# Moving the split tokens of a two-layer decoder trunk to multiples of 2048 bytes in SBUF

## The reference

```
for i in range(DEPTH):                       # DEPTH = 2
    y = swa_sink_attention(x, ...) if i % 2 == 0 else forgetting_attention(x, ...)
    x = layer_norm(ALPHA * x + y, ln_g[i, 0], ln_b[i, 0])
    h = causal_conv3(x @ w_up[i]) + conv_b[i]          # 2048 -> 2 * 5632 columns
    y = (silu(h[:, :5632]) * h[:, 5632:]) @ w_down[i]  # 5632 -> 2048 columns
    x = layer_norm(ALPHA * x + y, ln_g[i, 1], ln_b[i, 1])
```

## Time and profile before

| | |
|---|---|
| median of 3 runs | 2227.64 us (2227.63 to 2227.85) |
| profiled execution, its own time | 2227.25 us |
| its span, first to last instruction | 2225.4 us |
| TensorE busy | 2194.1 us (99%) |
| VectorE, ScalarE, GpSimd busy | 1336.2, 1039.6, 219.6 us |
| mean granted clock of TensorE | 0.996 |
| DMA queue of the weights | 385.92 MB, 56.5% of 16 engines |

### The profile page before, as it was taken

The page is one execution under the profiler, slowest core; times in us unless marked ns, Lnnn a source line. Parts: engine busy times, 40 slices in busy tenths (PEclk is TensorE's granted clock), DMA queues, the critical chain, the costliest instruction groups (busy, mean ns, idle before and its releaser), DMA issues.

```text
span 2225.4 us, 40894 instructions
## 1 busy us (share of the span) xinstructions
PE 2194.1 (99%) x15265; PEld 2027.2 (91%) x15265; DVE 1336.2 (60%) x1805; ACT 1039.6 (47%) x1380; POOL 219.6 (10%) x206
## 2 busy tenths in 40 slices
PE   8999999999999999999999999999999999999996
PEld 7998899999999988888899998899999999988885
DVE  5566576666666554446665665576666566654445
ACT  4554365454545443335444444364545454543332
POOL 2000002310000000000240330001230000000001
PEclk9999999999999999999999999999999999999998
DMA  8444556666666655555655654656666666665553
GB/s 262 152 149 157 180 163 206 199 198 188 187 186 187 187 188 188 189 186 158 189 183 163 203 172 140 196 160 196 201 203 187 188 188 188 186 225 187 187 188 104
DMA packets 206952, 408.71 MB, mean 184 GB/s; under 512 B 12652, under 2 KB 13756, under 8 KB 206620
## 3 DMA queue, kind: packets, MB, share of 16 engines
q1 hardware_dynamic: 200192, 385.92, 56.5%
q0 software_dynamic: 5776, 21.34, 3.1%
q10 hardware_dynamic: 908, 0.43, 0.1%
HBM read 405.46 MB, written 2.18 MB: 183 GB/s over the span
## 4 chain that ended last, share of the span: by engine, by line
PE 94%; DVE 3%; DMA 1%; ACT 1%; issue 0%; SPq 0%; ACTq 0%; DVEq 0%
PE ps L1176 19%; PE ps L1179 18%; PE ps L1178 18%; PE ps L1162 11%; PE ps L1164 11%; PE ps L1163 11%; PE ps L1304 1%; PE ps L1311 1%; DVE w_lo L749 1%; PE ps L1322 1%; PE ps L1323 1%; PE ps L1303 1%; PE ps L1321 0%; DMA raw<-in_a_w_qkv_dram 0%; DMA raw<-in_b_w_qkvf_dram 0%
## 5 line engine op out<-in xcount | busy, mean ns | idle before, releaser
L749 DVE TENSOR_TENSOR w_lo<-raw,w_hi 128x1024 fp32r<-128x1024 f32 x728 | 924.4, 1276 | 662.5 <-ACT w_hi L471 662.0
L471 ACT ACTIVATE w_hi<-raw 128x1024 fp32r<-128x1024 f32 x728 | 771.6, 1060 | 989.0 <-PE ps L1179 550.5
L1176 PE MATMUL ps<-xh,w_lo 128*128 128x256 f32 x3572 | 1006.3, 282 | 2.4 <-DVE xl L790 1.7
L1179 PE MATMUL ps<-xh,w_hi 128*128 128x256 f32 x3572 | 996.2, 279 | 0.0
L1178 PE MATMUL ps<-xl,w_hi 128*128 128x256 f32 x3572 | 996.2, 279 | 0.0
L1176 PEld LDWEIGHTS ps<-xh,w_lo 128*128 128x128 f32 x3572 | 671.7, 188 | 5.4 <-DVE xl L790 3.1
L1178 PEld LDWEIGHTS ps<-xl,w_hi 128*128 128x128 f32 x3572 | 671.9, 188 | 0.4
L1179 PEld LDWEIGHTS ps<-xh,w_hi 128*128 128x128 f32 x3572 | 671.4, 188 | 0.0
L1164 PE MATMUL ps<-w_hi,hid_h 128*128 128x512 f32 x704 | 278.4, 396 | 0.0
L1162 PE MATMUL ps<-w_lo,hid_h 128*128 128x512 f32 x704 | 278.4, 396 | 0.0
L1163 PE MATMUL ps<-w_hi,hid_l 128*128 128x512 f32 x704 | 278.4, 396 | 0.0
(11 more groups left out here) (164 smaller groups left out, 1501.1 us busy)
## 6 DMA issues: line engine op xcount, KB each, us to landing
raw<-in_ffn_w_up_dram SPq DMA_DIRECT2D x352, 512.0 KB, 3.6
raw<-in_ffn_w_down_dram SPq DMA_DIRECT2D x176, 512.0 KB, 4.4
raw<-in_b_w_qkvf_dram SPq DMA_DIRECT2D x96, 512.0 KB, 4.2
raw<-in_a_w_qkv_dram SPq DMA_DIRECT2D x40, 512.0 KB, 4.3
raw<-in_a_w_o_dram SPq DMA_DIRECT2D x32, 512.0 KB, 4.5
raw<-in_b_w_o_dram SPq DMA_DIRECT2D x32, 512.0 KB, 4.6
bias<-rel_by_distance POOLq DMA_DIRECT2D x4, 1024.0 KB, 6.6
bias<-minus_cumulated_decay POOLq DMA_DIRECT2D x4, 1024.0 KB, 6.8
```

The costliest lines, as they stand in the source:

```text
L471: act.activation(w_hi[:, loc % RING], raw[:, loc % RING], ACT.Copy).then_inc(high_ready, 1)
L749: dve.tensor_tensor(w_lo[:, s], raw[:, s], w_hi[:, s].bitcast(FP32), ALU.subtract).then_inc(low_ready, 1)
L1176: pe.matmul(o, w_lo[:, slot, k % 2, cols], xh[:, k, :], start=(k == 0 and j % 2 == 0), stop=False, skip_group_check=True)
L1179: last = pe.matmul(o, w_hi[:, slot, k % 2, cols], xh[:, k, :], start=False, stop=(k == KT - 1), skip_group_check=True)
```

## The change

One tile of 408 float32 per partition (1632 bytes) is declared behind `warm` and ahead of `xh`. Nothing reads or writes it.

More of the change, by code:

```diff
@@ L154, in trunk @@
         warm = sb("warm", [P, 1])
+        sb("fill", [P, 408])
         with ExitStack() as first:
```

## The result

| | before | after |
|---|---|---|
| median of the runs | 2227.70 us | 2245.49 us (2245.38 to 2245.62) |
| ratio, 95% interval | | 1.008 [1.0064, 1.0096] |
| span of the profiled execution | 2225.4 us | 2243.8 us |
| TensorE busy | 2194.1 us | 2213.0 us |
| VectorE, ScalarE busy | 1336.2, 1039.6 us | 1336.9, 1039.1 us |

The forecast was 2227.6 us with a range of 2168 to 2232. The first answer of the profile after is its busy times, which answer to the earlier trace rows.

What follows compares the result with a forecast made beforehand. The prediction took TensorE to bound the kernel, busy 2194.1 of 2225.4 us. All terms were 0: 2227.25 us of the profiled execution + 0, with the runs' median 0.4 us above, gave 2227.6 us, range 2168 to 2232.

Steps and rivals of the forecast that it cites:

- the small matmuls: Attention and transposes, an estimated 1000 matmuls: aligned or not they take the same, 0 us, bounds +-3 us.
- the step of 3.33 ns between neighbouring paces: Turned matmuls (256 moving columns): one cycle more per 32 columns, 36 for 35; used for the upper bound, +58.2 us.
- Reads of the big matmuls: Operand reads of 10752 turned (256 moving columns) and 3360 512-column matmuls: start addresses cost nothing, 0 us.
- rival 3: 14112 big matmuls: with both operands at 0 modulo 128, weight load strikes the moving read's memory; +58.2 us, 2285.8; chance 0.14.
- Rival 1: Big matmuls: reads clash less when starts differ by a multiple of 64, 34 cycles not 35; gain 58.2 us, 2169.4; chance 0.14.
- Rival 2: Big matmuls: the offset of 32 makes float32r slower than its columns; gain 130 us, 2098 us; chance 0.05.

Runs made afterwards that it cites:

- the bench: Runs of matmuls alone on idle memory, no layers computed, in stretches differing in operand starts, columns, types or leading matmuls; 256 moving columns at distance 0 took 120.0 ns.
- m1: Float32r matmuls alone on idle memory instead of the layers, 70 stretches of 48 with varied operand starts and columns; 256 moving columns took 120.0 ns at distance 0.
- e5: Against the kernel before: unused tiles of 160 bytes ahead of `xh` and 64 bytes ahead of `oh`; 2176.35 us, ratio 0.977.
- e2: Unused tile ahead of `xh` of 1760 bytes instead of the changed kernel's 1632 (distance 0 in both kinds); 2240.47 us, ratio 1.0055 to the kernel before.

## Why the prediction was wrong

**What held.** TensorE sets the time, no instruction changed, and VectorE, ScalarE and the small matmuls don't mind the addresses. After the change VectorE's and ScalarE's busy times are within 0.7 us of before, and the spacings of the small matmuls add up to the same within 0.1 us. The count of the big matmuls and their pace of before were right, and the step of 3.33 ns between neighbouring paces is a real one.

**The step that failed: "Reads of the big matmuls", taken as 0.** It measured +18.3 us (19.0 through the means): 20.8 lost on the turned matmuls, 2.5 gained on the others. The 0 rested on two readings of rows.

The first was that the extra cycles grow with the moving columns (24 for 256, 48 for 512), so that they are a share and not a price of a start. The two numbers are right, but the proportion was chance: the kernel had distance 32 with 256 columns and 224 with 512, which happen to give 24 and 48. In the bench the proportion holds at distance 32 by itself, and not at others: distance 224 has 28 and 48, distance 0 has 32 for both lengths (120.0 and 226.7 ns) and distance 192 has 16 and 48. Two points at two different distances were read as one law.

The second was the gate's products: the first eight at the pace of the turned matmuls, then 113 ns. I took the change of pace under equal addresses for proof that addresses have no part. They were equal modulo 128 only: `wf_hi` and `wf_lo` have 128 bytes per row tile, so the distance alternates between 64 and 192 modulo 256 from one k to the next. And by the nanosecond the first eight spacings are 116 to 120 ns, the ninth is 114, and all further ones are 113.3 in the mean: the stream settles into another cycle behind the turned matmuls. The bench shows the like: the stretch at distance 192 starts with 120, 117 and 115 ns before it stays at 113.3. So a pace that changes under like matmuls doesn't speak against addresses. A sign for them was in the rows: the same moving tiles ran at two steady paces with two stationary operands, though these differ in columns (128 and 32) as well as in address.

The constant mean over all column blocks and row tiles, which stood against rival 3, was no evidence either: those starts are multiples of 512 bytes apart, and distances that differ by 256 bytes or a multiple of it gave the same spacing (m1).

**The rivals.** Rival 1 (distances that are a multiple of 64 are good) had the size right and the condition wrong: 0, 64 and 128 are slower than 32 for the turned kind, and of the multiples of 64 only 192 gives 113.3 ns. Its 2169 us is near what e5 reached with other tiles' starts. Rival 3 named the right place and sign. Its price, one cycle per 32 columns in both kinds, was the step for the turned kind at distance 0 (120.0 ns, as in e2); at 128 it was 2.0 ns of 3.3, and the 512-column kind gained. Rival 2 (the whole overhead goes) has no support: no distance is under 113.3 and 226.7 ns.

**The two rules that the prediction weighed.** The formula of the Trainium skill's "TensorE: Matmul & The Clock Gate", section "Back-to-back issue gap", given there for an isolated matmul, fits bfloat16 back to back here (109.2 and 215.8 ns measured); no float32r stretch of 256 or 512 columns came under 113.3 and 226.7. The rule of two read ports of their own (the Trainium skill, same page, section "Step-by-step: what each phase is for") led to the wrong conclusion for float32r: where the two operands lie to each other changed the spacing, from 116.7 to 118.7 ns here. No run shows whether the ports themselves are at fault.

**What stays open.** Which part of the chip makes the 16 to 56 extra cycles of a 256-column matmul, how the matmuls ahead pick among the cycles of one distance, and why the list of good distances is irregular (113.3 ns at 112 and 192, 119.9 to 120.0 at 108, 116, 184 and 196). The runs show that the addresses' distance is the cause of the 17.8 us, and its period; the mechanism they don't show.

## What to carry to other kernels

For streams of float32r matmuls, compute the start of the moving operand less that of the stationary one modulo 256 bytes, and measure the spacing at a few such distances for the moving and stationary columns in use; 64 bytes of unused tile gave 2263.88 us here, 160 gave 2181.35, and 160 with another 64 further on gave 2176.35. A round start (a multiple of 2048) is no better than another, and 256- and 512-column matmuls want different distances, so pad tiles that serve as moving operands and tiles that serve as stationary ones separately. Measure in the kernel as well, since the work ahead of a stream can pick another cycle. When a steady pace differs from the columns' own time, two numbers taken at two different address pairs don't make a law.

## What the runs showed of the hardware that I had not expected

- The pace of back-to-back float32r matmuls with 128 stationary columns depends on the distance of their two operands: from 113.3 to 130.3 ns for 256 moving columns and from 226.7 to 236.8 ns for 512, at a granted clock of 1.00 throughout.
- bfloat16 and plain float32 show none of it over six distances each (109.2 ns for 256 columns of bfloat16, 215.8 for a record of plain float32).
- For some distances two steady cycles exist, and a few matmuls ahead decide between them (233.33 or 232.4 ns at distance 128 with 512 columns, 113.33 or 117.78 at 192 with 256). With 32 stationary columns the same products at the same addresses took 113.3 ns in one kernel and 120.0 in another.
- With 256 moving columns even one stationary column leaves 16 extra cycles on each float32r matmul (113.3 ns).
